# Modulation columns of each expert retrieval loaded in the stage before it, into a buffer of their own

## The chip, the cores and the metric

The kernel runs on one core of a Trainium2 chip, in one launch. The metric is the device time of that launch in microseconds. Three executions of the kernel before took 5094.03, 5090.95 and 5105.49 us; their median is 5094.03 us.

## What is computed

The program is a backbone of two layers over 512 latent tokens and a prefix of 256 context tokens, 1024 features each, all in float32. Each layer has two sub-layers, and each sub-layer first modulates its input per feature with a shift and a scale that come from the conditioning vector, as `h = x * (1 + scale) + shift`:

- a token mixer (pooling branch, bidirectional state-space scan, gates, output projection), which uses the modulation rows 0 (shift), 1 (scale) and 2 (gate);
- an expert retrieval (PEER), which uses rows 3 (shift), 4 (scale) and 5 (gate). It projects `h2 = x * (1 + sc2) + sh2` to queries, scores them against 2 x 128 keys for each of 8 heads, takes the 16 best pairs of keys for each head and token, fetches those experts' rows (8 KB each: an input row and an output row of 1024 floats) and sums their outputs.

Each sub-layer ends in `x = LayerNorm(alpha * x + gate * sublayer)`. The last layer needs no context output, so there are three retrievals in all: context in layer 0, latent in layer 0, latent in layer 1. The modulation rows of a layer and stream are 6 x 1024 floats in a DRAM tensor `mod_rows`, which the kernel itself fills in earlier stages.

## The kernel before

The program is a row of stages, each a `Block` that holds one instruction list for each engine; all engines meet at the end of a Block. Their order is: modulation rows, context projection, context scan, context outputs, **context merge** (`stage_merge`), **context retrieval** (`stage_peer`), reload, latent scan, latent outputs, **latent finish** (`stage_finish`, the merge of latent layer 0, whose projections were made ahead), **latent retrieval**, then for layer 1 the context return and scan, latent projection, scan, outputs, **latent merge** and the **last retrieval**. So each of the three retrievals follows a merge or finish stage of the same stream and layer, and these write the residual rows (`residual`) that the retrieval reads.

A retrieval Block has threads that a function `weave` puts into each engine's list by hand-written due times; at run time the order is fixed and only semaphores decide when an instruction starts. The parts that matter here:

- **SP** (the DMA queue) issues first the load of the 2 x 8 modulation columns of each partition (L1887: `mods[3D:5D]`, 8 KB in single floats, counted on `cols_loaded`), then the keys (L1889, 1 MB, counted on `loaded`). If the Block also projects the next mixer's input ahead (`ahead`, in both layer 0 retrievals) it issues three more loads counted on `cols_loaded`: the columns of the next mixer (L1891, again single floats), its convolution taps (L1893) and a weight (L1894). Then come the 1 MB weight blocks.
- **DVE** (VectorE) waits until `cols_loaded` has all of them, 16 where there is no ahead work and 64 where there is (L1961), and adds 1 to the scale columns (L1962).
- **PE** (TensorE) turns the residual through the identity, feature tile by feature tile, into two PSUM banks (L2180); from the third tile on it waits for the bank. After the eighth tile is modulated and the keys have landed it starts the 16 query products (L2196), and each product's scores (L2171).
- **ACT** (ScalarE) waits for DVE's addition (L2061, `consts_set`), and then reads each turned tile from its bank, multiplies by 1 + scale, adds the shift and writes `h2T` (L2065).
- **POOL** (GpSimd) starts the expert loads (L1946, an indirect DMA of 1 MB each, 128 rows of 8 KB) into a ring of 8 slots at the start of `arena`; a slot is free when PE has used it (L2297).

In the merge Block, SP issues the pooling weights, the inverse counts and three broadcast rows (L1055 to L1059) and then only weight blocks as their slots come free (L258). DVE clears buffers, takes the low parts of the modulated input (`modulate_rest`, L353), takes a reciprocal (L1181), scales `zs` (L1185) and goes on to the pooling windows (L1191 onward), for which it waits for all five loads and for ACT's copies. In the finish Block SP issues 16 tiles of 256 KB and three rows; DVE scales `zs`, takes low parts (L1620), waits for the loads and then for the first product (L1637).

On-chip memory is laid out by hand: each buffer takes the next place, rounded up to 32 bytes. The order at the end is `identity`, `triangles`, `ones`, `fold`, `iota`, `eps`, `cond_silu`, `pick_stream`, `final_states`, `arena`. With the sizes in the code, `arena` starts at byte 93,696 of each partition, and `norm_rows`, into which the keys are loaded (8 KB a partition), at byte 73,856.

Of the kernel before, what the change touches and what calls it, by code (L numbers as in the profile page):

```python
# [29 lines left out]
ALU = mybir.AluOpType  # L30
# [4 lines left out]
P = 128  # L35
D = 1024
KT = D // P
# [29 lines left out]
RING = 8  # L67
# [7 lines left out]

A_HT, A_XTOK, A_BT, A_CT, A_BTOK, A_ZS, A_HIN, A_SCR, A_ROWS = 0, 4096, 8192, 10240, 12288, 14336, 18432, 24576, 32000
A_TMP = A_HIN + 4096
ARENA = A_ROWS + PC_N + HR_N + KT * 32 + 16 + 4 * 288 + 480 - 184


PRE_WORDS = {2: 7200 + 96, 4: 512 + 64 + 16 + 96 + 256}
# [21 lines left out]
def setup(nc, ctx, io):  # L103
# [25 lines left out]
    k.ones = sb("ones", [P, P])  # L129
    k.fold = sb("fold", [P, QUAD])  # L130
    k.iota = sb("iota16", [P, TOPK])
    k.eps = sb("eps", [P, 1])
    k.csil = sb("cond_silu", [P, KT, 32])
    k.pick = sb("pick_stream", [P, 2])
    k.hfin = sb("final_states", [P, 2, D])
    k.arena = sb("arena", [P, ARENA])
    split = lambda name, at: alias(name, [P, KT, SEQ], "arena", at)[:]
# [879 lines left out]
def stage_merge(k, layer, stream, w0):  # L1017
# [34 lines left out]
    with nc.Block() as block:  # L1052
        @block.sync
        def _(sp):
            sp.dma_start(pool_w, io["pool_w"][layer]).then_inc(k.loaded.sem, 16)  # L1055
            ic = (io["icnt_grid"] if grid else io["icnt_line"])
            sp.dma_start(icnt, ic.unsqueeze(0).to_broadcast([P, 4, T])).then_inc(k.loaded.sem, 16)
            for dst, src in ((g1row, mods[2 * D:3 * D]), (lng, io["ln_g"][layer, 0]), (lnb, io["ln_b"][layer, 0])):
                sp.dma_start(dst, src.unsqueeze(0).to_broadcast([P, D])).then_inc(k.loaded.sem, 16)  # L1059
            load_wides(k, sp, w0 + n_wide + WIDE_SLOTS)  # L1060
            sp.wait_ge(k.loaded.sem, ld + 80)

# [112 lines left out]
        def _(dve):  # L1175
            nc.vector.memset(pa, 0.0)
            nc.vector.memset(ra, 0.0)
            nc.vector.memset(rb, 0.0)
            modulate_rest(k, dve, v, k.act_b, T)
            dve.wait_ge(k.rms_ready.sem, k.rms_ready.at(1))  # L1180
            nc.vector.reciprocal(rinv[:, 0:NT], rms[:, 0:NT])  # L1181
            dve.drain()
# [82 lines left out]
            for n in range(4 * NT):  # L1265
# [7 lines left out]
                if n >= 3 * NT:  # L1273
                    layer_norm(k, dve, k.res[:, tb + t], stats, lng, lnb, t)
    k.loaded.advance(80)
    k.rms_ready.advance(1)
    for x in (k.pin_copied, k.mixed_ready, k.pin_proj):
        x.advance(4)
# [240 lines left out]
def stage_finish(k, layer, w0):  # L1519
# [20 lines left out]
    with nc.Block() as block:  # L1540
        @block.sync
        def _(sp):
            for m in range(8):
                sp.dma_start(merged[:, m], io["pre_part"][m]).then_inc(k.reloaded[0].sem, 16)
            for m in range(8):
                sp.dma_start(sgs[:, m], io["pre_gs"][m]).then_inc(k.reloaded[1].sem, 16)
            for dst, src in ((g1row, mods[2 * D:3 * D]), (lng, io["ln_g"][layer, 0]), (lnb, io["ln_b"][layer, 0])):
                sp.dma_start(dst, src.unsqueeze(0).to_broadcast([P, D])).then_inc(k.loaded.sem, 16)
            load_wides(k, sp, w0 + n_wide + WIDE_SLOTS)
            sp.wait_ge(k.loaded.sem, ld + 48)  # L1550

# [58 lines left out]
        @block.vector  # L1610
        def _(dve):
            dve.wait_ge(k.rms_ready.sem, k.rms_ready.at(1))
            nc.vector.reciprocal(rinv[:, 0:NT], rms[:, 0:NT])
            dve.drain()
            for t in range(NT):
                y = v.zs[:, t].rearrange("p (g c) -> p g c", g=GROUPS)
                nc.vector.tensor_tensor(y, y, bc(rinv[:, t], [P, GROUPS, GW]), ALU.mult).then_inc(k.yn_ready.sem, 1)
            for kt in range(KT):
                dve.wait_ge(k.y_hi.sem, k.y_hi.at(kt + 1))
                nc.vector.scalar_tensor_tensor(k.act_b[:, kt, 0:T], k.ps[:, 6 + kt % 2, 0:T],  # L1620
                                               v.pcols[:, PC_NORM + kt:PC_NORM + kt + 1],
                                               k.act_a[:, kt, 0:T].bitcast(F32), ALU.mult, ALU.subtract) \
                    .then_inc(k.yt_copied.sem, 1)
            dve.wait_ge(k.reloaded[0].sem, P0 + 128)
            dve.wait_ge(k.reloaded[1].sem, G0 + 128)
            dve.wait_ge(k.loaded.sem, ld + 48)

            def merged_rest(m):

                dve.wait_ge(k.merged_hi.sem, k.merged_hi.at(m + 1))  # L1630
                nc.vector.tensor_tensor(k.act_e[:, m, 0:T], merged[:, m, 0:T], k.act_c[:, m, 0:T].bitcast(F32),
                                        ALU.subtract).then_inc(k.merged_lo.sem, 1)

            for m in range(8):
                dve.wait_ge(k.ys_proj.sem, k.ys_proj.at(m + 1))
                dve.drain()
                nc.vector.tensor_tensor(tmp[:, 0:T], k.ps[:, 2 + m % 2, 0:T], sgs[:, m, 0:T], ALU.mult)  # L1637
                dve.drain()
                nc.vector.tensor_tensor(merged[:, m, 0:T], merged[:, m, 0:T], tmp[:, 0:T], ALU.add) \
                    .then_inc(k.merged1.sem, 1)  # L1640
                if m >= 1:
                    merged_rest(m - 1)
            merged_rest(7)
            for n in range(4 * NT):
                t, quarter = n % NT, slice((n // NT) * WIDE, (n // NT + 1) * WIDE)
                dve.wait_ge(k.mix_proj.sem, k.mix_proj.at(n + 1))
                dve.drain()
                nc.vector.tensor_tensor(tmp[:, 0:WIDE], k.ps[:, n % 2, 0:WIDE], g1row[:, quarter], ALU.mult).then_inc(k.mix_read.sem, 1)
                dve.drain()
                x = k.res[:, tb + t, quarter]  # L1650
                nc.vector.scalar_tensor_tensor(x, x, ALPHA, tmp[:, 0:WIDE], ALU.mult, ALU.add)
                if n >= 3 * NT:
                    layer_norm(k, dve, k.res[:, tb + t], stats, lng, lnb, t)
    k.loaded.advance(48)
    k.reloaded[0].advance(128)
    k.reloaded[1].advance(128)
    k.rms_ready.advance(1)
# [8 lines left out]

def peer_views(k, NT):
    v = Bag()
    ring, h2T, scores, lhs, small, spare, modc, pre = carve(k, RING * 2 * D, NT * D, NT * 2048, 8 * QUAD, 2536, D, 16,
                                                            PRE_WORDS[NT])  # L1670
    v.ring = ring.rearrange("p (s c) -> p s c", s=RING)
    v.h2T = h2T.rearrange("p (t c) -> p t c", t=KT)
# [1 line left out]
    v.qT = spare.rearrange("p (a b) -> p a b", a=2)  # L1674
    v.keys = k.rows[:].rearrange("p a (m c) -> p (a m) c", c=P)
    v.lhs = lhs.rearrange("p (q j c) -> p q j c", q=4, j=NJ)
    v.modc = modc.rearrange("p (a t) -> p a t", a=2)
    v.small = small
    if NT == 2:
        v.hT = pre[:, 0:4096].rearrange("p (t c) -> p t c", t=KT)  # L1680
# [162 lines left out]
def stage_peer(k, layer, stream, w0, last_stage, ahead=False):  # L1843
# [40 lines left out]
    with nc.Block() as block:  # L1884
        @block.sync
        def _(sp):
            sp.dma_start(v.modc, mods[3 * D:5 * D].rearrange("(a t p) -> p a t", a=2, p=P),  # L1887
                         allow_slow_non_contiguous=True).then_inc(k.cols_loaded.sem, 16)
            sp.dma_start(v.keys, io["keys"][layer]).then_inc(k.loaded.sem, 16)  # L1889
            if ahead:  # L1890
                sp.dma_start(v.modh, io["mods"][ahead_layer, ahead_stream, 0:2 * D].rearrange("(a t p) -> p a t", a=2, p=P),  # L1891
# [66 lines left out]
        def _(dve):  # L1958
            def queries():
                yield 0.0  # L1960
                dve.wait_ge(k.cols_loaded.sem, k.cols_loaded.at(64 if ahead else 16))  # L1961
                nc.vector.tensor_scalar(v.modc[:, 1], v.modc[:, 1], 1.0, None, ALU.add).then_inc(k.consts_set.sem, 1)  # L1962
                for m in range(M):
                    yield proj_at(m + 2) + 1.0
                    dve.wait_ge(k.s_proj.sem, nth(k.s_proj, m + 1))
                    dst = v.scores.rearrange("p (t c) -> p t c", t=NT)[:, :, m * P:(m + 1) * P]
                    nc.vector.tensor_copy(dst, k.ps[:, 5 + m % 2, 0:T].rearrange("p (t c) -> p t c", c=P)) \  # L1967
                        .then_inc(k.s_copied.sem, 1)

            def project():  # L1970
                yield PRE
                dve.wait_ge(k.cols_loaded.sem, k.cols_loaded.at(64))
                nc.vector.tensor_scalar(v.modh[:, 1], v.modh[:, 1], 1.0, None, ALU.add).then_inc(k.consts_set.sem, 1)
                yield item_at(1) + 0.5
                dve.wait_ge(k.pre["evac"].sem, pre0["evac"] + 1)
# [82 lines left out]
        def _(act):  # L2058
            def queries():
                yield 0.0  # L2060
                act.wait_ge(k.consts_set.sem, k.consts_set.at(1))  # L2061
                for kt in range(KT):
                    yield PROJ / KT * (kt + 1)
                    act.wait_ge(k.xt_ready.sem, nth(k.xt_ready, kt + 1))
                    nc.scalar.activation(v.h2T[:, kt, 0:T], k.ps[:, 2 + kt % 2, 0:T], ACT.Identity,  # L2065
                                         bias=v.modc[:, 0, kt:kt + 1], scale=v.modc[:, 1, kt:kt + 1]) \
                        .then_inc(k.h_ready.sem, 1)
                for m in range(M):
                    yield proj_at(m + 1) + 0.5
# [4 lines left out]

            def project():
                yield PRE + 1.0
                act.wait_ge(k.consts_set.sem, k.consts_set.at(2))
                for kt in range(KT):
                    yield PRE + 1.5 * (kt + 1)
                    act.wait_ge(k.pre["turn"].sem, pre0["turn"] + kt + 1)  # L2080
# [83 lines left out]
        def _(pe):  # L2164
# [46 lines left out]
            def project():  # L2211
# [9 lines left out]
                    last.then_inc(k.pre["turn"].sem, 1)  # L2221
                yield item_at(0)
                pe.wait_ge(k.pre["h"].sem, pre0["h"] + KT)
                pe.wait_ge(k.cols_loaded.sem, k.cols_loaded.at(64))
                for t in range(AN):
                    for kt in range(KT):
                        last = nc.tensor.matmul(k.ps[:, 5, t * 32:(t + 1) * 32], v.hT[:, kt, t * P:(t + 1) * P], v.wdt[:, kt],
# [80 lines left out]

            weave(queries(), retrieve(), *([project()] if ahead else []))
    k.loaded.advance(64)  # L2310
    k.cols_loaded.advance(64 if ahead else 16)
    k.consts_set.advance(2 if ahead else 1)
    if ahead:
        for i in range(4):
            k.pre_kept[i].advance(16 * sum(1 for e in range(ITEMS) if keep_of(e) == i))
        for name, count in (("turn", KT), ("h", KT), ("proj", ITEMS), ("evac", ITEMS), ("pad", 1), ("conv", PRE_SCAN),
# [116 lines left out]
```

## Time and profile before

| | us |
|---|---|
| three executions, median | 5094.03 |
| lowest, highest | 5090.95, 5105.49 |
| the profiled execution, device time | 5106.41 |
| its span, first to last instruction | 5104.6 |
| busy in it: PE / DVE / POOL / ACT | 3574.8 / 3231.1 / 2228.7 / 1500.9 |

All rows below are of the profiled execution. An engine's busy time says little by itself here: the stages have different limits, and what an edit at the door of a stage is worth is read from the instructions at that door in order of time.

### The profile page before, as it was taken

The page shows a single profiled execution, that of the slowest core. Times are in us where ns is not written, and L with a number is a line of the kernel's source. Part 1 is how long each engine was busy: PE and PEld are TensorE (multiplying, and loading weights), DVE is VectorE, ACT ScalarE, POOL GpSimd, SP SyncE. Part 2 cuts the span into 40 slices and gives each one's busy share as a digit, 9 for nine tenths or more (in the row PEclk, how much of TensorE's full clock was granted, in tenths as well). Part 3 has the DMA queues.
Part 4 walks back from the last instruction along what each step waited for, and adds up shares of the span by engine and source line. Part 5 has one row for each costly group of instructions (what it writes and reads, how often), then busy time and mean ns, then how long its engine had stood idle before and what let it go on. Part 6 is the DMA issues. An engine that isn't in the chain of part 4 may idle for free. (4 is left out here: it accounts for less than half of the span.)

```text
span 5104.6 us, 48751 instructions
## 1 busy us (share of the span) xinstructions
PE 3574.8 (70%) x15800; PEld 1819.3 (36%) x15800; DVE 3231.1 (63%) x6592; ACT 1500.9 (29%) x3675; POOL 2228.7 (44%) x1683
## 2 busy tenths in 40 slices
PE   7888888887677896555555556979897555555555
PEld 5676424322276442111111115877742111111111
DVE  5255776764465467777776766466446677777675
ACT  2342334343242234222222223243222222222221
POOL 3253444443033244555555552333324555555554
PEclk9888999998788998877777777889998777777777
DMA  5435999998703599999999992102269999999998
GB/s 179 173 112 209 394 373 411 382 426 365 268 1 112 217 378 412 416 411 420 401 425 413 410 417 89 68 1 91 83 238 368 414 416 413 418 410 419 411 416 370
DMA packets 251726, 1575.59 MB, mean 309 GB/s; under 512 B 42560, under 2 KB 49216, under 8 KB 65472
## 3 DMA queue, kind: packets, MB, share of 16 engines
q0 software_dynamic: 184320, 1342.26, 63.8%
q1 hardware_dynamic: 67152, 230.23, 12.4%
q8 instruction: 125, 2.05, 0.1%
q14 instruction: 129, 1.06, 0.1%
HBM read 1554.88 MB, written 17.50 MB: 308 GB/s over the span
## 5 line engine op out<-in xcount | busy, mean ns | idle before, releaser
L2297 PE MATMUL banks<-arena 128*64 128x512 f32 x5120 | 1631.6, 776 | 1174.1 <-ACT arena L2148 1173.2
L1946 POOL DMA_INDIRECT arena<-in_experts,arena x1280 | 1514.7, 1183 | 1650.7 <-PE banks L2297 1393.0
L2034 DVE CUSTOM_DVE_ANT_0 arena<-arena,token_copies 128x1024 f32<-128x1024 f32 x1280 | 1647.9, 1304 | 684.9 <-DMA arena<-in_experts,arena 615.0
L2297 PEld LDWEIGHTS banks<-arena 128*64 128x64 f32 x5120 | 390.9, 169 | 2260.8 <-ACT arena L2148 1626.4
L2141 ACT ACTIVATE arena<-arena 128x2 f32<-128x2 f32 x640 | 131.2, 205 | 1808.7 <-DVE arena L2034 1797.0
L281 POOL TENSOR_TENSOR wide_low<-wide_blocks,wide_high 128x1024 fp32r<-128x1024 f32 x136 | 342.8, 2543 | 556.4 <-ACT wide_high L271 556.4
L2148 ACT ACTIVATE arena<-arena 128x64 f32<-128x64 f32 x1280 | 376.0, 340 | 300.0 <-POOL arena L1820 259.6
L2196 PE MATMUL banks<-arena,wide_blocks 128*128 128x512 f32 (+1 forms) x768 | 296.1, 531 | 2.6 <-ACT arena L2065 2.6
L319 PE MATMUL banks<-activation_a,wide_high 128*128 128x512 f32 (+1 forms) x768 | 278.2, 362 | 8.5 <-ACT arena L343 2.7
L2249 PE MATMUL banks<-arena,wide_blocks 128*128 128x512 f32 x576 | 277.5, 619 | 0.0
L321 PE MATMUL banks<-activation_a,wide_low 128*128 128x512 f32 (+1 forms) x768 | 269.2, 351 | 0.0
L854 POOL COPY arena<-arena 128x512 f32<-128x512 f32 x80 | 63.7, 810 | 405.5 <-SPq L838 298.5
L1778 POOL TENSOR_TENSOR arena<-arena 128x512 f32<-128x512 f32 x80 | 109.2, 1365 | 214.9 <-DVE arena L1759 213.4
L2196 PEld LDWEIGHTS banks<-arena,wide_blocks 128*128 128x128 f32 x768 | 141.1, 193 | 124.9 <-issue 114.9
L320 PE MATMUL banks<-activation_b,wide_high 128*128 128x512 f32 (+1 forms) x512 | 180.6, 353 | 0.0
L2141 ACT ACT_TABLE_LOAD x131 | 168.1, 1283 | 4.2
L271 ACT CAST wide_high<-wide_blocks 128x1024 fp32r<-128x1024 f32 x136 | 135.4, 1045 | 104.3 <-PE banks L319 46.1
L1820 POOL TENSOR_TENSOR arena<-fold,arena 128x1024 f32<-128x1024 f32 x80 | 158.5, 1981 | 13.0 <-ACT arena L1812 11.5
L2249 PEld LDWEIGHTS banks<-arena,wide_blocks 128*128 128x128 f32 x576 | 104.5, 194 | 167.3 <-issue 163.1
L319 PEld LDWEIGHTS banks<-activation_a,wide_high 128*128 128x128 f32 x768 | 150.7, 196 | 30.8 <-ACT arena L343 3.5
L321 PEld LDWEIGHTS banks<-activation_a,wide_low 128*128 128x128 f32 x768 | 150.4, 196 | 19.2
L1967 DVE COPY arena<-banks 128x512 f32<-128x512 f32 (+1 forms) x48 | 28.7, 600 | 198.2 <-PE banks L2171 172.6
(248 smaller groups left out, 5055.8 us busy)
## 6 DMA issues: line engine op xcount, KB each, us to landing
wide_blocks<-in_wide SPq DMA_DIRECT2D x168, 1024.0 KB
arena<-in_experts,arena POOLq DMA_INDIRECT x1280
pre_scan<-arena SPq DMA_DIRECT2D x16, 256.0 KB
arena<-pre_scan SPq DMA_DIRECT2D x16, 256.0 KB, 5.2
residual<-in_tokens SPq DMA_DIRECT2D x6, 512.0 KB
arena<-mod_rows SPq DMA_DIRECT2D x6, 512.0 KB
norm_rows<-in_keys SPq DMA_DIRECT2D x3, 1024.0 KB
pre_z<-arena SPq DMA_DIRECT2D x8, 256.0 KB
```

The lines of the kernel that those rows point to most:

```text
L281: k.nc.gpsimd.tensor_tensor(k.wide_lo[:, n % WIDE_SLOTS, rows], k.wide[:, n % WIDE_SLOTS, rows], k.wide_hi[:, n % HI_SLOTS, rows].bitcast( ...
L319: signal_used(k, nc.tensor.matmul(out, lh, rh, start=(kt == 0), stop=False))
L320: nc.tensor.matmul(out, lh, rl, start=False, stop=False)
L321: last = nc.tensor.matmul(out, ll, rh, start=False, stop=(kt == KT - 1))
L1820: nc.gpsimd.tensor_tensor(masks, k.fold[:].unsqueeze(1).to_broadcast(shape), bc(gate[:, u % 2].rearrange("p s j -> p (s j)"), shape), ALU. ...
L1946: pool.indirect_dma_start(out=v.ring[:, g % RING], out_offset=None, in_=io["experts"], in_offset=bass.IndirectOffsetOnAxis(ap=c.idx[:, u % ...
L2034: last = nc.vector.tensor_tensor_reduce(out=u_row, in0=u_row, in1=k.copies[:, n % NJ], scale=1.0, scalar=0.0, op0=ALU.mult, op1=ALU.add, a ...
L2141: nc.scalar.activation(c.gel[:, a:a + NJ], c.act_in[:, a:a + NJ], ACT.Gelu_apprx_tanh)
L2148: last = nc.scalar.activation(v.lhs[:, g % 4, j], c.masked[:, q * NJ + j], ACT.Copy, scale=c.gel[:, a + j:a + j + 1])
L2196: last = nc.tensor.matmul(k.ps[:, 2 + m % 2, 0:T], k.wide[:, n % WIDE_SLOTS, kt, (m % 2) * P:(m % 2 + 1) * P], v.h2T[:, kt, 0:T], start=(k ...
L2249: last = nc.tensor.matmul(k.ps[:, 5 + e % 2, 0:AT], w[:, kt, (e - 1) % 2 * P:((e - 1) % 2 + 1) * P], v.hT[:, kt], start=(kt == 0), stop=(k ...
L2297: mm = nc.tensor.matmul(k.ps[j * QUAD:(j + 1) * QUAD, a + half], v.lhs[:, g % 4, j], v.ring[:, (g * NJ + j) % RING, D + half * BANK:D + (h ...
```

## The change

1. A buffer `nextmod` (`peer_modulation`, 2 x 8 floats a partition) is added. `eps` and `pick` now share one buffer of three floats, and the retrieval's `modc` leaves the arena, which is declared 16 words smaller. By the sizes in the code, `arena` then starts at byte 93,728 of each partition, and what lay behind `modc` in a retrieval's views moves 64 bytes down within it.
2. The load of the columns (`mods[3D:5D]`) leaves the start of `stage_peer` and is issued in `stage_merge` and `stage_finish`, behind the three broadcast rows and ahead of the weight blocks.
3. The addition of 1 leaves `stage_peer`'s DVE list. In `stage_merge` DVE does it behind `modulate_rest`, in `stage_finish` behind its waits for the loads; each waits for the columns' load first.
4. ACT's wait for that addition is gone from the retrieval; `cols_loaded` there counts only the three ahead loads (48 instead of 64, none without ahead work).

```diff
@@ setup
-ARENA = A_ROWS + PC_N + HR_N + KT * 32 + 16 + 4 * 288 + 480 - 184
+ARENA = A_ROWS + PC_N + HR_N + KT * 32 + 16 + 4 * 288 + 480 - 200
...
-    k.eps = sb("eps", [P, 1])
+    k.trio = sb("eps_and_pick", [P, 3])
+    k.eps, k.pick = k.trio[:, 0:1], k.trio[:, 1:3]
     k.csil = sb("cond_silu", [P, KT, 32])
-    k.pick = sb("pick_stream", [P, 2])
+    k.nextmod = sb("peer_modulation", [P, 2, KT])
@@ stage_merge, SP (and the same two lines in stage_finish, SP)
             for dst, src in ((g1row, mods[2 * D:3 * D]), (lng, io["ln_g"][layer, 0]), (lnb, io["ln_b"][layer, 0])):
                 sp.dma_start(dst, src.unsqueeze(0).to_broadcast([P, D])).then_inc(k.loaded.sem, 16)
+            sp.dma_start(k.nextmod[:], mods[3 * D:5 * D].rearrange("(a t p) -> p a t", a=2, p=P),
+                         allow_slow_non_contiguous=True).then_inc(k.cols_loaded.sem, 16)
             load_wides(k, sp, w0 + n_wide + WIDE_SLOTS)
@@ stage_merge, DVE
             modulate_rest(k, dve, v, k.act_b, T)
+            dve.wait_ge(k.cols_loaded.sem, k.cols_loaded.at(16))
+            nc.vector.tensor_scalar(k.nextmod[:, 1], k.nextmod[:, 1], 1.0, None, ALU.add)
             dve.wait_ge(k.rms_ready.sem, k.rms_ready.at(1))
@@ stage_finish, DVE
             dve.wait_ge(k.loaded.sem, ld + 48)
+            dve.wait_ge(k.cols_loaded.sem, k.cols_loaded.at(16))
+            nc.vector.tensor_scalar(k.nextmod[:, 1], k.nextmod[:, 1], 1.0, None, ALU.add)
@@ stage_peer, SP
-            sp.dma_start(v.modc, mods[3 * D:5 * D].rearrange("(a t p) -> p a t", a=2, p=P),
-                         allow_slow_non_contiguous=True).then_inc(k.cols_loaded.sem, 16)
             sp.dma_start(v.keys, io["keys"][layer]).then_inc(k.loaded.sem, 16)
@@ stage_peer, DVE
-                dve.wait_ge(k.cols_loaded.sem, k.cols_loaded.at(64 if ahead else 16))
-                nc.vector.tensor_scalar(v.modc[:, 1], v.modc[:, 1], 1.0, None, ALU.add).then_inc(k.consts_set.sem, 1)
...
-                dve.wait_ge(k.cols_loaded.sem, k.cols_loaded.at(64))
+                dve.wait_ge(k.cols_loaded.sem, k.cols_loaded.at(48))
@@ stage_peer, ACT
-                act.wait_ge(k.consts_set.sem, k.consts_set.at(1))
...
                     nc.scalar.activation(v.h2T[:, kt, 0:T], k.ps[:, 2 + kt % 2, 0:T], ACT.Identity,
-                                         bias=v.modc[:, 0, kt:kt + 1], scale=v.modc[:, 1, kt:kt + 1]) \
+                                         bias=k.nextmod[:, 0, kt:kt + 1], scale=k.nextmod[:, 1, kt:kt + 1]) \
```

## Rows read from the trace of the kernel before

**Rows 1.** The page: span, and the DMA queue of the expert loads.

```profile
span 5104.6 us, 48751 instructions
...
q0 software_dynamic: 184320, 1342.26, 63.8%
```

**Rows 2.** Windows, last retrieval: length, busy PE, PEld, DVE, ACT, POOL, clock, DMA share, GB/s.

```profile
3900.00:4300.00 400.00, 220.92 (x776) 59.96 (x776) 289.31 (x676) 97.41 (x292) 221.88 (x178) 0.75 1.00 415
```

**Rows 3.** Timeline, context retrieval's start: start us, duration us, engine, line [idle before <-releaser].

```profile
428.62 0.38 SPq L1887 DMA_DIRECT2D arena<-mod_rows  x1
...
428.67 1.09 PE L2180 MATMUL banks<-identity,residual 128*128 128x128 f32 x4 [8.82 <-PEq L1052]
...
437.45 0.17 DVE L1962 TENSOR_SCALAR arena<-arena 128x8 f32<-128x8 f32 x1 [9.08 <-DMA arena<-in_w_dt]
437.66 1.02 ACT L2065 ACTIVATE arena<-banks,arena 128x256 f32<-128x256 f32 x2 [12.13 <-DVE arena L1962]
...
438.27 1.15 PE L2180 MATMUL banks<-identity,residual 128*128 128x128 f32 x4 [8.51 <-ACT arena L2065]
...
439.00 1.02 ACT L2065 ACTIVATE arena<-banks,arena 128x256 f32<-128x256 f32 x2 [0.32 <-PE banks L2180]
...
442.77 9.11 PE L2196 MATMUL banks<-arena,wide_blocks 128*128 128x256 f32 x32 [0.65 <-ACT arena L2065]
```

**Rows 4.** Timeline, start of the latent retrieval of layer 0.

```profile
1663.66 1.94 PE L2180 MATMUL banks<-identity,residual 128*128 128x128 f32 x8 [13.34 <-PEq L1540]
...
1672.12 1.45 ACT L2065 ACTIVATE arena<-banks,arena 128x512 f32<-128x512 f32 x2 [11.51 <-DVE arena L1962]
...
1672.95 5.94 PE L2180 MATMUL banks<-identity,residual 128*128 128x128 f32 x24 [7.34 <-ACT arena L2065]
1674.10 1.63 ACT L2065 ACTIVATE arena<-banks,arena 128x512 f32<-128x512 f32 x2 [0.54 <-PE banks L2180]
...
1679.76 14.00 PE L2196 MATMUL banks<-arena,wide_blocks 128*128 128x512 f32 x32 [0.87 <-ACT arena L2065]
```

**Rows 5.** Timeline, start of the last retrieval.

```profile
3704.48 1.94 PE L2180 MATMUL banks<-identity,residual 128*128 128x128 f32 x8 [13.38 <-PEq L1052]
...
3707.58 1.45 ACT L2065 ACTIVATE arena<-banks,arena 128x512 f32<-128x512 f32 x2 [5.89 <-DVE arena L1962]
...
3715.00 14.00 PE L2196 MATMUL banks<-arena,wide_blocks 128*128 128x512 f32 x32 [1.10 <-ACT arena L2065]
```

**Rows 6.** Windows at the three starts: the keys' last bytes, and the three rises of the clock.

```profile
434.00:435.00 1.00, 0.00 (x0) 0.00 (x0) 0.00 (x0) 0.00 (x0) 0.00 (x0) 0.50 0.95 281
...
446.00:448.00 2.00, 2.00 (x9) 1.71 (x8) 0.00 (x0) 0.00 (x0) 0.00 (x0) 0.82 0.00 0
...
1678.00:1680.00 2.00, 1.13 (x6) 0.73 (x5) 0.00 (x0) 1.56 (x2) 0.00 (x0) 0.77 0.00 0
...
3713.00:3714.00 1.00, 0.90 (x7) 0.52 (x5) 0.00 (x0) 0.69 (x2) 0.00 (x0) 0.86 0.00 0
```

**Rows 7.** Timeline of the merges and the finish stage: DVE at the addition's place, one SP load.

```profile
298.05 0.20 DVE L1181 RECIPROCAL arena<-arena 128x8 f32<-128x8 f32 x1
...
1543.91 0.43 SPq L1548 DMA_DIRECT2D arena<-mod_rows  x1
...
1563.96 0.69 DVE L1637 TENSOR_TENSOR arena<-banks,arena 128x512 f32<-128x512 f32 x1 [5.51 <-PE banks L321]
...
3465.49 0.25 DVE L1181 RECIPROCAL arena<-arena 128x16 f32<-128x16 f32 x1
```

**Rows 8.** Windows in which the merges' loads end.

```profile
294.00:295.00 1.00, 0.69 (x2) 0.29 (x2) 0.45 (x2) 1.00 (x4) 0.00 (x0) 0.50 0.45 168
...
3461.00:3462.00 1.00, 1.00 (x4) 0.60 (x4) 0.56 (x1) 1.00 (x2) 0.00 (x0) 0.50 0.43 156
```

**Rows 9.** Waits in the last merge (3452 to 3704): total us, times, longest.

```profile
DVE arena L1238 <- PE banks L1096: 46.4, 8, 6.2
```

**Rows 10.** Window, last retrieval's start, in which the keys alone are loaded (into `norm_rows`).

```profile
3708.00:3709.00 1.00, 0.58 (x3) 0.59 (x4) 0.00 (x0) 1.00 (x2) 0.00 (x0) 0.50 0.99 418
```

More of the change, by code:

```diff
@@ L1275, in stage_merge @@
     k.loaded.advance(80)
+    k.cols_loaded.advance(16)
     k.rms_ready.advance(1)
@@ L1548, in _ @@
                 sp.dma_start(dst, src.unsqueeze(0).to_broadcast([P, D])).then_inc(k.loaded.sem, 16)
+            sp.dma_start(k.nextmod[:], mods[3 * D:5 * D].rearrange("(a t p) -> p a t", a=2, p=P),
+                         allow_slow_non_contiguous=True).then_inc(k.cols_loaded.sem, 16)
             load_wides(k, sp, w0 + n_wide + WIDE_SLOTS)
@@ L1654, in stage_finish @@
     k.loaded.advance(48)
+    k.cols_loaded.advance(16)
     k.reloaded[0].advance(128)
@@ L1668, in peer_views @@
     v = Bag()
-    ring, h2T, scores, lhs, small, spare, modc, pre = carve(k, RING * 2 * D, NT * D, NT * 2048, 8 * QUAD, 2536, D, 16,
+    ring, h2T, scores, lhs, small, spare, pre = carve(k, RING * 2 * D, NT * D, NT * 2048, 8 * QUAD, 2536, D,
                                                             PRE_WORDS[NT])
@@ L1676, in peer_views @@
     v.lhs = lhs.rearrange("p (q j c) -> p q j c", q=4, j=NJ)
-    v.modc = modc.rearrange("p (a t) -> p a t", a=2)
     v.small = small
@@ L2076, in project @@
                 yield PRE + 1.0
-                act.wait_ge(k.consts_set.sem, k.consts_set.at(2))
+                act.wait_ge(k.consts_set.sem, k.consts_set.at(1))
                 for kt in range(KT):
@@ L2223, in project @@
                 pe.wait_ge(k.pre["h"].sem, pre0["h"] + KT)
-                pe.wait_ge(k.cols_loaded.sem, k.cols_loaded.at(64))
+                pe.wait_ge(k.cols_loaded.sem, k.cols_loaded.at(48))
                 for t in range(AN):
@@ L2310, in stage_peer @@
     k.loaded.advance(64)
-    k.cols_loaded.advance(64 if ahead else 16)
-    k.consts_set.advance(2 if ahead else 1)
     if ahead:
+        k.cols_loaded.advance(48)
+        k.consts_set.advance(1)
         for i in range(4):
```

## The prediction

> **What bounds the kernel now.** The page's queue table comes first: the expert loads take 63.8% of what the 16 DMA engines have in 5104.6 us, some 3257 us [rows 1]. A window well inside the last retrieval shows the DMA engines busy all the time, at 415 GB/s, with every compute engine having room [rows 2]. So a retrieval's length behind its first expert load is set by how many bytes it fetches, which the change leaves alone. What can be had is the time ahead of that first load, in which the DMA engines are nearly idle. For that I read the instructions in order of time at the three retrievals' starts, and then the places in the merge and finish stages to which the work goes.
>
> At the context retrieval's start PE turns its first tiles at 428.67, and then ACT is idle until 437.66: it waits for DVE's addition, and that for the last of four loads (to L1894's weight), whose data ACT does not need yet [rows 3]. At the latent start of layer 0 it is the same, from 1663.66 to 1672.12 [rows 4]. In the last retrieval there are no ahead loads, only the columns': 3704.48 to 3707.58 [rows 5]. PE has two banks and stands as long.
>
> **The change part by part.**
>
> *The wait at the door.* Without it ACT starts when a tile is turned. How long that takes is in the same rows. In the context stage PE resumes at 438.27 and ACT reads at 439.00, 0.73 us later [rows 3], so ACT's first instruction would come at 428.67 + 0.73 = 429.40, 8.26 us before 437.66. With 512 tokens PE resumes at 1672.95 and ACT reads at 1674.10, 1.15 us [rows 4]: 1663.66 + 1.15 = 1664.81, 7.31 us before 1672.12. In the last one 3704.48 + 1.15 = 3705.63, 1.95 us before 3707.58 [rows 5]. From ACT's first instruction to the first query product it is 5.11, 7.64 and 7.42 us [rows 3 to 5]; that ping-pong of PE and ACT keeps its form, since the second tile is turned while the first is modulated. Products would start at 434.5, 1672.5 and 3713.05. Sum: 8.26 + 7.31 + 1.95 = 17.5 us.
>
> *What is late next: the keys.* PE's products also wait for the keys. Before, their last bytes move in the window 434 to 435, behind 2,048 single floats of columns [rows 6]. Without those the keys are issued at 428.6 instead of about 429.1, and their bytes, 1 MB at 418 GB/s [rows 10], take 2.5 us. Bounds: landing near 432.5 (no loss), or as late as before less the issue of 0.38 us that is gone [rows 3], near 434.6, which would cost 0.1 to 0.5 us in this stage. In the other two the products come later behind the start (8.8 and 8.6 us) and nothing is lost. I take 0.
>
> *The clock.* The granted clock is at 0.5 (1.2 GHz) at each start and then rises to 1.0 (2.4 GHz). The share in the rising window gives the moment: 0.82 in 446 to 448 is 446.7, 0.77 in 1678 to 1680 is 1678.9, 0.86 in 3713 to 3714 is 3713.3 [rows 6]. So before, 3.9 us of context products ran at the lower level, none of the others. PE ran with a gap of 7 to 8 us in the first two cases; in the third, with a gap of 2 us, the rise came 8.8 us after the first turned tile. If it comes 8.8 us after it everywhere, it falls at 437.5, 1672.5 and 3713.3: 3.0 us of slow products in context, 0 to 0.2 elsewhere, a gain of 0.4 us. If it keeps the old dates, slow products last 12.2, 6.4 and 0.3 us, that is 8.3 + 6.4 + 0.3 = 15.0 us more at half pace, a loss of 7.5 us. The last start is nearest to the new form (hardly a gap), so I stay near the small end and take a loss of 0.5 us.
>
> *The load in the merges.* It is 8 KB behind 2.5 MB (context), 3 MB (last merge) or 5.5 MB (finish) already in the queue. In the merges those bytes end at 294.45 and 3461.4 (a window's share 0.45 and 0.43) [rows 8]. The single floats then need 1 to 2 us and a landing: 296 to 297.5, and 3463 to 3464.5. DVE reaches the place of the wait at 298.05 and 3465.49 [rows 7], so it does not stop. If it did by 3 us, there are behind it the reciprocal, the scaling of `zs`, and the pooling windows; these feed PE's L1096, for which DVE itself waits 46.4 us in the last merge [rows 9], so the delay ends there and PE doesn't see it. In the finish stage the first of the three row loads is issued at 1543.91 [rows 7], so the columns follow at about 1545.3; even if none of the 5.5 MB had moved by then, at 415 GB/s they would be through 13.3 us later, at 1558.6, and DVE stands idle from 1558.45 to 1563.96 [rows 7]. SP has nothing to issue behind it but weight blocks whose slots are still in use; the addition is 0.17 us [rows 3], in DVE's idle time. All of it: 0, at worst 0.2 us.
>
> *What goes.* One load, one addition and a wait less in each retrieval, all counted above. DVE's ahead thread now waits for three loads, long before it needs them.
>
> *The arena moves by 32 bytes,* from a multiple of 512 to 93,728. The ring lies at its start, so every 8 KB row of the expert loads ends up across 33 blocks of 256 bytes instead of 32. The nearest row is the keys' load: it goes to byte 73,856, which is 128 beyond a multiple of 256, also 8 KB a partition and across 33 blocks. It flows at 418 GB/s at a DMA share of 0.99 [rows 10], the aligned expert loads at 415 at 1.00 [rows 2]. No cost shows, so I take 0; an offset of 32 itself no row shows, and the upper end is one block in 32 more, 3257 / 32 = 102 us.
>
> The Trainium skill (DMA: Bandwidth & Descriptors, "How a descriptor splits into AXI transactions") says that a descriptor that doesn't start at a multiple of 256 bytes costs a further transaction. It speaks of reading; the expert rows are read from multiples of 8 KB in either kernel, so by it nothing changes there. Taken for the writing side, it would have charged the keys' load too, which the trace doesn't show.
>
> **Sum.** 17.5 - 0.5 = 17.0 us. The profiled execution took 5106.4 us, so it would take 5089.4; it lies 12.4 us above the median of the runs. The stages at issue don't scale with that, so from 5094.0 the forecast is 5077.0 us.
>
> **The rivals.**
>
> 1. *The clock keeps its dates.* For it: the first two rises come 8.4 and 6.0 us after PE resumes behind its gap, not after its first tile [rows 3, 4, 6]. Against: the gap goes, so PE is busy earlier. It gives 17.5 - 7.5 = 10.0 us, 5084.
> 2. *The head start is lost in the retrieval.* Expert loads start sooner, but the ring, the ahead projections and the weight blocks meet in another phase, and the retrieval ends when it did. For it: POOL, DVE and PE wait for each other in turn at every slot. Against: a DMA share of 1.00 leaves no slack in which a head start could be lost [rows 2]. 5094.
> 3. *The displaced ring makes it slower.* The place is each expert row's write into the ring. From the point at which a row takes 17.0 / 3257 = 0.52% longer, the change is a loss; one block in 32 gives 5077 + 102 = 5179 us. For it: the DMA engines have no slack, so every per cent is paid in full [rows 1, 2]. Against: rows 10.
> 4. *The door was not the wait* (ACT goes on to be held, by its own code load for instance). Then nothing moves. Rows 3 to 5 name the releaser at all three doors and PE starts at once there; I count it with rival 2.
>
> **How the numbers follow.** Forecast 0.65, rival 1 0.13, rival 2 with 4 0.12, rival 3 0.10. The forecast's own range is 5068 to 5087: 17 us, with the keys' 0.5, and runs of one kernel that lie up to 11 us apart from their median. With rivals 1 and 2 it is 5066 to 5096; rival 3 is left out. A measurement of this kernel can tell a difference of about 0.3%, 15 us, from none, and the forecast lies just beyond that: three quarters of its chance fall beyond it, 0.48; the rest of it and rivals 1, 2 and 4 are no change, 0.42; rival 3 is slower, 0.10.
>
> **What would show it.** In the changed kernel's rows, ACT's first L2065 line of each retrieval lies 0.7 to 1.2 us behind PE's first turned tile, instead of 9.0, 8.5 and 3.1 us; the first query product 5.8 to 8.8 us behind it. The first expert load of each retrieval is earlier by the same amount, and the distance from it to the stage's end is unchanged. DVE's idle time at the addition in the merges is below 1 us. The clock's rise is 8 to 9 us behind the first turned tile; if it is at 14 us or more, rival 1 is right. If the DMA share stays 1.00 at under 410 GB/s in the last retrieval's middle, it is rival 3. The forecast is wrong if products start early and the expert loads don't.

## The result: 0.27% slower, though all three waits went as forecast

The changed kernel takes 5114.21 us (median of 20 runs, 5100.89 to 5124.86) against 5099.81 us before (20 runs, 5083.53 to 5108.11). The ratio is 1.0027 with a 95% interval of 1.0018 to 1.0035, so it is 9 to 18 us slower. I had forecast 17 us faster, and the time lies outside the range of 5066 to 5096. (A ratio is the recorded one, which is not exactly the ratio of the two medians: in the runs below the two differ by up to 0.12%.)

The doors of the three retrievals come first. This is the timeline of the changed kernel (start us, duration us, engine, line [idle before <-releaser]); L2185 turns the tiles, L2070 is ACT's modulation and L2201 the query products.

```profile
423.99 1.09 PE L2185 MATMUL banks<-identity,residual 128*128 128x128 f32 x4 [8.43 <-PEq L1053]
424.69 1.02 ACT L2070 ACTIVATE arena<-banks,peer_modulation 128x256 f32<-128x256 f32 x2 [3.48 <-PE banks L2185]
...
429.80 9.05 PE L2201 MATMUL banks<-arena,wide_blocks 128*128 128x256 f32 x32 [0.66 <-ACT arena L2070]
...
1654.93 4.64 PE L2185 MATMUL banks<-identity,residual 128*128 128x128 f32 x20 [13.39 <-PEq L1546]
...
1656.06 1.63 ACT L2070 ACTIVATE arena<-banks,peer_modulation 128x512 f32<-128x512 f32 x2 [3.91 <-PE banks L2185]
...
1662.78 14.00 PE L2201 MATMUL banks<-arena,wide_blocks 128*128 128x512 f32 x32 [0.87 <-ACT arena L2070]
...
3703.52 3.77 PE L2185 MATMUL banks<-identity,residual 128*128 128x128 f32 x16 [13.04 <-PEq L1053]
3704.65 1.63 ACT L2070 ACTIVATE arena<-banks,peer_modulation 128x512 f32<-128x512 f32 x2 [3.91 <-PE banks L2185]
...
3711.21 14.00 PE L2201 MATMUL banks<-arena,wide_blocks 128*128 128x512 f32 x32 [0.87 <-ACT arena L2070]
```

ACT now starts 0.70, 1.13 and 1.13 us behind the first turned tile; what it waits for is PE. The first query product comes 5.81, 7.85 and 7.69 us behind the tile, where it was 14.10, 16.10 and 10.52 [rows 3 to 5]. That is 8.3 + 8.3 + 2.8 = 19.4 us won, and it reaches the first expert load: it lies 35.5, 46.3 and 46.2 us behind the first tile instead of 43.9, 54.5 and 49.0.

The time is lost behind that. Here are the page's span and its line on the expert loads' queue (packets, MB, share of 16 engines), which answer to [rows 1]:

```profile
span 5109.5 us, 48748 instructions
...
q0 software_dynamic: 184320, 1342.26, 64.3%
```

Summed from the packet records, the same packets and bytes took 3285.3 us of the 16 engines' time instead of 3258.4: 26.9 us more, in a resource that has no room through most of the latent retrievals. The window of the last retrieval, which answers to [rows 2], says it as a rate: the share is 1.00 as before, at 411 GB/s instead of 415.

```profile
3900.00:4300.00 400.00, 223.06 (x768) 61.12 (x768) 282.59 (x663) 97.28 (x291) 217.20 (x177) 0.75 1.00 411
```

In the two latent retrievals the issues of the 512 expert loads (min/median/max ns, first to last start) spread wider. Before:

```profile
L1946 POOL DMA_INDIRECT arena<-in_experts,arena x512: 932/938/2033, 1718.2 to 3062.6; - x171
...
L1946 POOL DMA_INDIRECT arena<-in_experts,arena x512: 932/938/2022, 3753.5 to 5076.9; - x171
```

After:

```profile
L1954 POOL DMA_INDIRECT arena<-in_experts,arena x512: 932/938/1994, 1701.2 to 3057.0; - x171
...
L1954 POOL DMA_INDIRECT arena<-in_experts,arena x512: 932/938/2003, 3749.7 to 5081.1; - x171
```

1344.4 became 1355.8 and 1323.4 became 1331.4 us, 19.4 us together, where PE, DVE and POOL have room in both kernels. The context retrieval's 256 issues spread over 771.1 us instead of 766.8. That closes the balance of the profiled pair: the spans differ by 4.9 us, so 19.4 + 4.9 = 24.3 us are lost behind the doors, and the three spreads account for 11.4 + 8.0 + 4.3 = 23.7 of them.

The trace's packet records show what changed. Of the 163,840 expert rows of 8 KB, 1% before and 65% after took between 310 and 330 ns; 96% and 32% took 309, and 2 to 3% took longer than 330 in both. The mean went from 317.1 to 319.7 ns.

### The profile page after: what moved, and what is told of

Same layout as the page of the kernel before. It is cut to its first block and busy times, and to the rows that moved or that the text cites. A ratio compares the mean times of both kernels' runs of the same rounds, so it can differ in the third digit from the quotient of the medians.

```text
span 5109.5 us, 48748 instructions
## 1 busy us (share of the span) xinstructions
PE 3580.1 (70%) x15800; PEld 1821.2 (36%) x15800; DVE 3239.3 (63%) x6592; ACT 1501.4 (29%) x3675; POOL 2192.8 (43%) x1683
## 3 DMA queue, kind: packets, MB, share of 16 engines
q0 software_dynamic: 184320, 1342.26, 64.3%
## 5 line engine op out<-in xcount | busy, mean ns | idle before, releaser
L1954 POOL DMA_INDIRECT arena<-in_experts,arena x1280 | 1479.1, 1156 | 1708.5 <-PE banks L2302 1456.3
L2201 PE MATMUL banks<-arena,wide_blocks 128*128 128x512 f32 (+1 forms) x768 | 297.3, 533 | 2.4 <-ACT arena L2070 2.4
L2201 PEld LDWEIGHTS banks<-arena,wide_blocks 128*128 128x128 f32 x768 | 141.6, 193 | 125.3 <-issue 115.7
```

What stands on the lines that cost most here:

```text
L1954: pool.indirect_dma_start(out=v.ring[:, g % RING], out_offset=None, in_=io["experts"], in_offset=bass.IndirectOffsetOnAxis(ap=c.idx[:, u % ...
L2201: last = nc.tensor.matmul(k.ps[:, 2 + m % 2, 0:T], k.wide[:, n % WIDE_SLOTS, kt, (m % 2) * P:(m % 2 + 1) * P], v.h2T[:, kt, 0:T], start=(k ...
```

## The experiments

Theory D: the expert loads pay for the ring's new address, which the added buffer moved by 32 bytes. Its rivals: P, the head start gets lost in another phase of the retrieval; M, the work that was moved into the merges costs it. All ratios are against the kernel before on the same chip; three chips were used, and the kernel before's median on them was 5102.11 us (the first four experiments), 5109.82 (the next four) and 5098.28 (the last four). The two profile lines under four of the kernels are the page's line on the expert loads' queue and the window 3900 to 4900, which is DMA-bound in every kernel. Ring addresses are bytes in each partition.

### The kernel before, ring at 93,664 (32 beyond a multiple of 64)

```diff
-    k.eps = sb("eps", [P, 1])
...
     k.arena = sb("arena", [P, ARENA])
+    k.eps = sb("eps", [P, 1])
```

> The kernel before, with one edit: eps lies behind the arena, so that the arena (and the ring at its start) begins at byte 93,664, which is 32 beyond a multiple of 64, as 93,728 is in the changed kernel. No instruction differs. Theory D (the displaced ring makes the expert rows' packets longer): 20 to 30 us slower than before, ratio 1.004 to 1.006; the expert loads' share of the DMA engines rises from 63.8% to about 64.3%. Theory P (the head start of the change is lost in the retrieval by another phase of ring, ahead work and weight blocks): no difference, 1.000, since nothing starts earlier here. Theory M (the work moved into the merges costs it): no difference.

Measured: 5133.63 us, ratio 1.0067 (1.0050 to 1.0083), 34 us slower by the ratio and 32 by the medians, with not one instruction changed. This is D, somewhat dearer than expected; P and M can't give it.

```profile
q0 software_dynamic: 184320, 1342.26, 64.1%
...
3900.00:4900.00 1000.00, 547.39 (x1952) 152.07 (x1952) 728.01 (x1706) 242.87 (x730) 553.01 (x442) 0.75 1.00 413
```

The packet records sum to 3287.8 us, beside the changed kernel's 3285.3. The share is 64.1% and not the expected 64.3%, since the span, 5125.8 us, grew too.

### The change with the arena where it was, 93,696

```diff
-    k.nextmod = sb("peer_modulation", [P, 2, KT])
+    sb("gap", [P, 8])
...
     k.arena = sb("arena", [P, ARENA])
+    k.nextmod = sb("peer_modulation", [P, 2, KT])
```

> The changed kernel with its arena at byte 93,696, where it was before (the new buffer lies behind it). Theory D: what the waits at the three doors were worth is left, 17 to 20 us faster than before, ratio 0.996 to 0.997, expert loads at 63.8 to 63.9% of the DMA engines. Theory P: as the changed kernel, ratio 1.002 to 1.003. Theory M: the same, 1.002 to 1.003.

Measured: 5083.43 us, ratio 0.9963 (0.9949 to 0.9977), 19 us faster than before. Against the changed kernel's 1.0027 it is the arena's address alone, 0.64% or 33 us. P and M are out: the same instructions, loads and merges are here.

```profile
q0 software_dynamic: 184320, 1342.26, 64.0%
...
3900.00:4900.00 1000.00, 551.89 (x1968) 154.03 (x1968) 728.97 (x1713) 244.75 (x736) 560.92 (x445) 0.75 1.00 416
```

The packet records sum to 3255.1 us, about what they took before (3258.4); the share is above the expected 63.8 to 63.9% because the span is shorter.

### How coarse the grid is: 64 bytes

The kernel before with `iota` behind the arena (ring at 93,632, 64 short of where it was), and the changed kernel with 8 words ahead of the ring (93,760, 64 beyond a multiple of 256):

```diff
-    ring, h2T, scores, lhs, small, spare, pre = carve(k, RING * 2 * D, ...
+    _, ring, h2T, scores, lhs, small, spare, pre = carve(k, 8, RING * 2 * D, ...
```

> The kernel before with iota behind the arena, so that the arena begins at byte 93,632: a multiple of 64, 192 beyond a multiple of 256. No instruction differs. Theory D in its form with 64 bytes (only an offset that is no multiple of 64 costs): 1.000 against before. Theory D in its form with 256 bytes (33 blocks instead of 32): as slow as with 32 bytes, 1.004 to 1.006. Theories P and M: 1.000.

> The changed kernel, arena still at 93,728, but with 8 words ahead of the ring in the retrieval's views, so that ring and all buffers of the retrieval lie at a multiple of 64 (ring at 93,760, 64 beyond a multiple of 256) while the mixers' stages keep the displaced arena. Theory D with 64 bytes and the cost in the retrievals: 14 to 20 us faster than before, 0.996 to 0.997. If the cost sits in the mixers' stages (reload, merges): as the changed kernel, 1.002 to 1.003. Theory D with 256 bytes: as the changed kernel. Theories P and M: as the changed kernel.

Measured: 1.0027 (1.0014 to 1.0039) and 1.0024 (1.0012 to 1.0036). A multiple of 64 is not enough; both have 59% of their expert rows at 310 to 330 ns. My "64 bytes" was wrong. The first one lost only 15 us, less than the other displaced forms of the kernel before; why, I can't say, as its packets are as long as theirs, and its latent retrievals' issues spread as wide (1354.0 and 1332.3 us).

### Whose displacement it is: ring, other buffers, or mixers

The changed kernel three times, with 8 spare words and `eps_and_pick` or `peer_modulation` behind the arena: (a) ring at 93,696, all else of the retrieval 32 bytes further; (b) retrieval as before, mixers' buffers 32 bytes off; (c) mixers as before, ring at 93,728 with the rest of the retrieval.

```diff
-    ring, h2T, scores, ... = carve(k, RING * 2 * D, NT * D, ...          # the change
+    ring, _, h2T, scores, ... = carve(k, RING * 2 * D, 8, NT * D, ...    # (a), arena at 93,696
+    _, ring, h2T, scores, ... = carve(k, 8, RING * 2 * D, NT * D, ...    # (b), arena at 93,664; (c), at 93,696
```

> The changed kernel with arena and ring at byte 93,696 as before, and 8 words between the ring and the other buffers of the retrieval, so that these alone (turned input, scores, small buffers, ahead buffers) lie 32 bytes further. Theory R (the cost is the ring's own displacement, where the DMA engines write the expert rows): 17 to 20 us faster than before, 0.996 to 0.997, as with everything aligned. Theory O (the engines' operands at displaced addresses cost): about 1.000 to 1.002.

> The changed kernel with the arena at byte 93,664 (32 beyond a multiple of 64) and 8 words ahead of the ring, so that the ring and all of the retrieval lie where they lay before (ring at 93,696), and only the mixers' stages have displaced buffers. Theory R (the ring alone): 0.996 to 0.997. Theory X (the mixers' stages, with their own loads, share the cost; the kernel with the ring at a multiple of 64 and displaced mixers came out at 1.0024): 0.998 to 1.000, with the stretch between the context retrieval's last expert load and the latent door longer by 5 to 10 us.

> The changed kernel with the arena at byte 93,696 and 8 words ahead of the ring: the mixers' buffers lie as before, the ring and all of the retrieval 32 bytes further (ring at 93,728, its place in the changed kernel). Theory R: as the changed kernel, 1.001 to 1.003, the latent retrievals' expert loads lasting 8 to 11 us longer each than before. Theory X: between, 0.999 to 1.001.

Measured: (a) 5078.77 us, 0.9945 (0.9930 to 0.9959); (b) 5088.36 us, 0.9963 (0.9949 to 0.9977); (c) 5111.14 us, 1.0009 (1.0000 to 1.0018). With the ring in place, no cost shows of the retrieval's other buffers being displaced (a), nor of the mixers' (b), where a cost of 0.1 to 0.2%, 7 us or so, would be lost in the intervals: theory O falls, and by (b) theory X. With the ring displaced the gain is gone; on the same chip (c) takes 23 us more than (b) and 32 more than (a).

Not all of it came out as R had it. (c) lies just below R's 1.001 to 1.003, inside X's 0.999 to 1.001, and below the changed kernel's 1.0027 with the ring at the same address; why, the runs don't show. The kernel before was some 10 us slower on this chip than in the changed kernel's own comparison, while (c) and the changed kernel are 3 us apart. What speaks for R in (c) are its expert rows, as long as the changed kernel's (table below), and its latent issues, which spread over 1356.0 and 1335.2 us, 11.6 and 11.8 more than before. The stretch that X wanted longer in (b), from the context retrieval's last expert load to the latent door, was 430.7 us instead of 424.3. That doesn't speak for X: it was 430.7 in (c) too, whose mixers lie as before, and 434.1 with the ring at 93,440 below.

### The grid: 128, 256 or 512 bytes

The kernel before with small buffers behind the arena: `eps`, `pick` and `iota` (ring at 93,568), `fold` (93,440), `ones` (93,184), and `fold`, `eps`, `pick` and `iota` (93,312); each diff has the form of the first experiment's.

> The kernel before with eps, pick and iota behind the arena, so that the arena and the ring begin at byte 93,568: 128 beyond a multiple of 256. No instruction differs. Offsets of 32 and of 64 both cost. Theory G128 (what costs is not to begin at a multiple of 128; the keys, at such an address, flowed freely): 1.000, expert packets at 309 ns. Theory G256 (a multiple of 256 is needed): 1.003 to 1.005, packets of 311 to 313 ns again.

> The kernel before with fold behind the arena: arena and ring begin at byte 93,440, a multiple of 256 and not of 512. No instruction differs. Offsets of 32, 64 and 384 beyond a multiple of 512 cost 14 to 34 us. Theory G256 (any multiple of 256 is free): 1.000, expert packets at 309 ns. Theory G512 (a multiple of 512 is needed): 1.003 to 1.006, packets of 311 to 320 ns.

> The kernel before with ones behind the arena: arena and ring begin at byte 93,184, 512 bytes lower, again a multiple of 512. G256 and G512: 1.000 and packets at 309 ns. Theory A (any other order of the small buffers costs, whatever the address): 1.003 or more.

> The kernel before with fold, eps, pick and iota behind the arena: arena and ring begin at byte 93,312, 128 beyond a multiple of 512, which is the offset of the keys and the weight blocks, whose packets take 309 ns. If the offset alone decides, and 128 beyond 512 is free: 1.000 and 309 ns. If expert rows by the indirect loads pay at any address that is no multiple of 256 or 512, where the plain loads don't: 1.003 to 1.006, 311 to 321 ns.

| ring at | beyond a multiple of 512 | kernel | ratio (95%) | rows at 310 to 330 ns | mean ns |
|---|---|---|---|---|---|
| 93,696 | 0 | before | 1 | 1% | 317.1 |
| 93,184 | 0 | before | 1.0006 (0.9992 to 1.0019) | 1% | 316.7 |
| 93,440 | 256 | before | 1.0007 (0.9993 to 1.0022) | 1% | 316.8 |
| 93,568 | 384 | before | 1.0053 (1.0037 to 1.0069) | 44% | 319.5 |
| 93,312 | 128 | before | 1.0055 (1.0037 to 1.0073) | 42% | 319.3 |
| 93,632 | 448 | before | 1.0027 (1.0014 to 1.0039) | 59% | 319.3 |
| 93,664 | 480 | before | 1.0067 (1.0050 to 1.0083) | 67% | 319.9 |
| 93,696 | 0 | change, rest displaced | 0.9945 (0.9930 to 0.9959) | 1% | 317.0 |
| 93,696 | 0 | change | 0.9963 (0.9949 to 0.9977) | 1% | 316.8 |
| 93,696 | 0 | change, mixers displaced | 0.9963 (0.9949 to 0.9977) | 1% | 316.9 |
| 93,728 | 32 | change | 1.0027 (1.0018 to 1.0035) | 65% | 319.7 |
| 93,728 | 32 | change, mixers in place | 1.0009 (1.0000 to 1.0018) | 66% | 320.2 |
| 93,760 | 64 | change, ring 8 words on | 1.0024 (1.0012 to 1.0036) | 59% | 319.3 |

The line falls at 256: at its multiples no cost shows, whatever moved to get there, and each of the five other remainders tried (32, 64, 128, 192 and 224) costs. G256 holds; G128, G512 and A fall.

Where the cost falls is plain in the issues' spread over all fourteen kernels. In the first latent retrieval it is 1339.5 to 1349.0 us with the ring at a multiple of 256 and 1352.6 to 1361.0 elsewhere, in the last one 1314.2 to 1323.4 and 1331.0 to 1335.2. The means differ by 11 and 13 us. In the context retrieval, where PE is busy for 82 to 91% of each 100 us from 500 to 1200 before, the two groups overlap: 761.7 to 767.4 and 763.3 to 771.1. Here are the queue line and the window at 93,440:

```profile
q0 software_dynamic: 184320, 1342.26, 63.8%
...
3900.00:4900.00 1000.00, 549.73 (x1960) 152.41 (x1956) 721.33 (x1696) 247.01 (x736) 557.11 (x444) 0.75 1.00 417
```

and at 93,568:

```profile
q0 software_dynamic: 184320, 1342.26, 64.1%
...
3900.00:4900.00 1000.00, 546.75 (x1944) 149.75 (x1944) 729.78 (x1696) 245.30 (x730) 537.31 (x439) 0.75 1.00 412
```

The share alone hardly tells them apart, since the span grows with it; the rate in a saturated stretch does: 414 to 418 GB/s in all seven kernels with the ring at a multiple of 256, 410 to 413 in all seven others (windows 2000 to 3000 and 3900 to 4900 of each).

The Trainium skill (DMA: Bandwidth & Descriptors, "How a descriptor splits into AXI transactions") has this number: it says that a transaction moves at most 256 bytes and must start at a multiple of 256. By that, 8 KB from any other start take 33 transactions instead of 32. The runs agree on the 256, and show it at the writing end; that section of the Trainium skill speaks of what a transaction reads. They don't agree on the size: one in 32 more, an estimate from the Trainium skill's rule, would be 3% of a row, while the mean row grew by 0.7 to 1.0%, single rows by 0.6 to 4% and many not at all. No run counts transactions, so that they are the cause isn't shown.

### The witness: weight blocks and keys 32 bytes further, ring in place

```diff
+    k.eps = sb("eps", [P, 1])
     k.wide = sb("wide_blocks", [P, WIDE_SLOTS, KT, WIDE])
```

> The kernel before with eps ahead of the weight blocks: these, wide_high and the keys begin 32 bytes further (weight blocks at 41,120, keys at 73,888), the arena stays at 93,696. If plain loads pay for 32 bytes as the indirect ones do: the weight blocks' packets go from 309 to 313 to 320 ns; 0.27 MB per ns: 168 blocks of 1 MB at 1% more is 4 us at most in the sum of the DMA time, and within 0.1% of the time of the kernel. If they don't pay: packets at 309 ns, 1.000. The expert loads stay at 309 ns in either case.

Measured: 1.0013 (1.0000 to 1.0027), by the medians 2 us, which can't be told from nothing. The median of the plain loads' 8 KB packets is 309 ns as before, and beside the context retrieval's expert loads 98% of them are at 309 ns or less (96% before). So the plain loads don't pay for their own address at 128 or at 160 beyond a multiple of 256. They are no witness for the indirect ones. (In the expectation, "0.27 MB per ns" is a slip on which nothing rests: 168 MB at 415 GB/s take 405 us, and 1% of that is 4 us.)

They do pay for the ring's. In the stretch of the context retrieval's expert loads the records hold 3,456 plain packets of 8 KB, those of 27 weight blocks. In the seven kernels with the ring at a multiple of 256, this one among them, 1% of these took 310 to 330 ns. In the seven others it was 24 to 38% (38% in the changed kernel, 28% in the kernel before with the ring at 93,664), although the weight blocks lie where they lay. They pay in whole blocks, in the changed kernel 67 to 89% of the packets of eleven, at most 4% of ten, and 12 to 60% of six. So a displaced ring lengthens packets beside it too, and not only the rows that are written into it. This explains as little as before why a given packet is long, but it shows where plain loads can tell something: beside the loads at issue, and not alone.

## Why the prediction was wrong

The base lay low by chance: the median of three runs was 5094.03, that of twenty 5099.81. Moved up by 6 us the range would be 5072 to 5102, and 5114.21 is still outside.

**Waits at the doors: right.** 17.5 us forecast, 19.4 measured. The 0.73 and 1.15 us from tile to ACT were 0.70 and 1.13.

**Keys: right.** PE goes from the last tile to the first product in 0.66 to 0.87 us of idle time, released by ACT.

**Clock: the size near, the rule wrong.** A loss of 0.5 us was forecast and none came: 3.8 us of context products ran at the lower level instead of 3.9. Windows at the three rises in the changed kernel:

```profile
432.00:434.00 2.00, 2.00 (x7) 1.59 (x7) 0.00 (x0) 0.00 (x0) 0.00 (x0) 0.59 0.00 0
...
1658.00:1660.00 2.00, 1.83 (x11) 1.19 (x10) 0.00 (x0) 1.88 (x3) 0.00 (x0) 0.75 1.06 209
...
3706.00:3708.00 2.00, 1.83 (x11) 1.33 (x9) 0.00 (x0) 1.65 (x3) 0.00 (x0) 0.75 0.76 320
```

By the shares it rose at 433.6, 1659.0 and 3707.0, that is 9.7, 4.1 and 3.5 us behind the first tile, not 8.8 everywhere. In the latent stages PE was busy without a gap from the first tile to the rise; in the context stage it paused 0.2 us between pairs of tiles, and the rise came 3.8 us after the first product. In the latent stages the last tiles were then turned at the upper level, and from ACT's first instruction to the first product it was 6.72 and 6.56 us instead of 7.64 and 7.42; these 1.8 us are nearly all of the 1.9 beyond the forecast. That one was luck: the forecast had the ping-pong keep its pace. Rival 1 is refuted.

**Work moved into the merges: right.** DVE in the changed kernel at the addition (L1184, L1636):

```profile
292.88 0.16 DVE L1184 TENSOR_SCALAR peer_modulation<-peer_modulation 128x8 f32<-128x8 f32 x1
...
1549.99 0.16 DVE L1636 TENSOR_SCALAR peer_modulation<-peer_modulation 128x8 f32<-128x8 f32 x1
...
3462.68 0.16 DVE L1184 TENSOR_SCALAR peer_modulation<-peer_modulation 128x8 f32<-128x8 f32 x1
```

No idle time stands before any of them: the columns had landed. The kernel with the arena in place has all of this and is 0.37% faster.

**The arena moves by 32 bytes: this step failed.** I wrote "No cost shows, so I take 0", because the keys' load at 128 beyond a multiple of 256 flowed at 418 GB/s [rows 10] against 415 of the aligned expert loads [rows 2]. Both rows are true and the inference is not. It compared a plain load, alone for 2.5 us, with indirect loads in a saturated stretch, and a plain load doesn't pay for its own address. With it fell the premise of the first paragraph, that behind the first expert load only the bytes count, and the sign "the distance from it to the stage's end is unchanged". In its place stands a cost that was put at 0: 0.27 to 0.67% of the time in the four displaced forms of the kernel before, and 0.64%, 33 us, between the changed kernel and its form with the arena in place, against the 19 us won. That 33 - 19 gives the measured 14 us is no check, since all three come from the same two ratios. A check is the kernel before with the ring at 93,664: its 34 us, less the 19.4 us read at the doors, give 15. Rival 3 had the place, the longer rows and the point of decision right (a row 0.52% longer turns the sign; it was 0.8%), at three times the price (102 us) and a chance of 0.10. Its count of 33 blocks instead of 32 isn't shown to be the reason. Its sign in the profile was set too low: I had asked for under 410 GB/s and it was 411.

**The early start is kept**, against rival 2: with the ring in place it comes out whole, as 19 us (12 to 26).

Not settled: why plain loads don't pay for their own address, and how a displaced ring lengthens packets beside it; why only some rows pay, and in stretches (in the changed kernel's last retrieval, in groups of 128 rows by start time, 5% of the first group, 84 to 95% of the ninth to fourteenth, at most 5% of the nine behind them, up to 98% later); and why the ring at 93,632 lost only 15 us with packets as long as at the others. The 24 us lost in the profiled execution are less than the 33 in the ratios: it is one execution each, the one before 7 us above its median and the one after 3 us below, and runs of one kernel lie up to 25 us apart.

## What to carry to other kernels

When an edit adds or resizes a buffer, work out the start address, modulo 256, of every buffer behind it, and above all of those into which a saturated indirect load writes. Fix that address by itself, with the small buffers behind it, so that later edits can't move it; here the same change is worth -0.37% with the ring in place and +0.27% without. A row from the trace excludes a cost only if it shows the same kind of load under the same pressure; where none does, try the address alone, since that experiment changes no instruction.

## What the runs showed of the hardware

- Indirect loads of 8 KB rows from DRAM: with the destination at a multiple of 256 bytes 309 ns for 95 to 96% of the packets; at 32, 64 and 128 bytes beside one, 42 to 67% of them took 310 to 330 ns, nearly all of these 311 to 316 or 318 to 321.
- Plain loads of 8 KB a partition, at 128 and at 160 bytes beyond a multiple of 256: 309 ns in the median.
- Beside the context retrieval's indirect loads, 1% of the plain 8 KB packets took 310 to 330 ns with the ring at a multiple of 256 and 24 to 38% with the ring elsewhere, at plain addresses that had not moved.
- No cost showed for operands of PE, DVE and ACT 32 bytes off: ratio 0.9945 with the retrieval's buffers other than the ring displaced, 0.9963 with the mixers' displaced (same chip), 0.9963 with nothing displaced (another chip).
- In the changed kernel's latent stages PE was idle for 13 us, then busy without a gap, and the granted clock rose from 0.5 to 1.0 4.1 and 3.5 us behind the first tile. In the context stage, with pauses of 0.2 us between pairs of tiles, it rose 9.7 us behind the first tile, 3.8 us behind the first product.
